# More expert-row dots among the query pieces, fewer behind them, and a smoother ramp of GpSimd's row requests

## The reference

```python
def peer_ffn(h, w_q, subkeys, u, v):
    def chunk(ht):
        q = (ht @ w_q).reshape(128, 8, 2, 128)
        s = jnp.einsum('thpc,hpnc->thpn', q, subkeys)
        sv, si = lax.top_k(s, 16)
        cand_s = sv[:, :, 0, :, None] + sv[:, :, 1, None, :]
        cand_i = si[:, :, 0, :, None] * 128 + si[:, :, 1, None, :]
        top_s, top_pos = lax.top_k(cand_s.reshape(...), 16)
        expert = jnp.take_along_axis(cand_i.reshape(...), top_pos, axis=-1)
        gate = jax.nn.softmax(top_s, axis=-1)
        act = gelu(jnp.einsum('thkd,td->thk', u[expert], ht))
        return jnp.einsum('thk,thkd->td', gate * act, v[expert])
    return lax.map(chunk, hc)
```

## Time and profile before

| | before |
|---|---|
| median of 3 runs | 2679.6 us (2672.1 to 2680.65) |
| the profiled execution | 2673.85 us, its span 2672.1 us |
| TensorE busy | 2589.0 us (97%) |
| VectorE busy | 2137.8 us (80%) |
| GpSimd busy | 1497.7 us (56%) |
| ScalarE busy | 883.2 us (33%) |
| moved by DMA | 763.33 MB |

### The profile page before, as it was taken

The page is one execution under the profiler, slowest core; times in us unless marked ns, Lnnn a source line. Parts: engine busy times, 40 slices in busy tenths (PEclk is TensorE's granted clock), DMA queues, the critical chain, the costliest instruction groups (busy, mean ns, idle before and its releaser), DMA issues.

```text
span 2672.1 us, 41571 instructions
## 1 busy us (share of the span) xinstructions
PE 2589.0 (97%) x15177; PEld 2324.3 (87%) x15177; DVE 2137.8 (80%) x4585; ACT 883.2 (33%) x1656; POOL 1497.7 (56%) x960
## 2 busy tenths in 40 slices
PE   7999989999999999999999999999999999999998
PEld 6777767999999999999999999987888788888886
DVE  6122273589888899999999996769898899989998
ACT  4223252222222222236666664222222222222222
POOL 1111020245666677776655656846776677767763
PEclk9999999999999999999999999999999999999999
DMA  4110023335777899999999999999999999999995
GB/s 149 48 32 25 24 62 121 111 107 166 266 271 268 295 318 325 319 328 365 385 373 380 383 372 375 406 359 366 388 383 387 370 385 385 387 386 376 385 375 220
DMA packets 296526, 763.33 MB, mean 286 GB/s; under 512 B 25808, under 2 KB 116304, under 8 KB 293584
## 3 DMA queue, kind: packets, MB, share of 16 engines
q0 software_dynamic: 110592, 402.70, 40.2%
q1 hardware_dynamic: 161280, 288.88, 31.3%
q10 hardware_dynamic: 24528, 70.26, 6.8%
HBM read 669.47 MB, written 92.27 MB: 285 GB/s over the span
## 4 chain that ended last, share of the span: by engine, by line
PE 61%; DVE 12%; DMA 7%; issue 4%; POOL 2%; ACT 1%; SPq 0%; DVEq 0%; ACTq 0%
PE bank L1659 27%; PE bank L2048 12%; PE wide L2048 9%; PE bank L2019 5%; DMA g_raw<-g_d 4%; PE bank L1879 3%; PE bank L1934 2%; DVE u_row L1393 2%; DMA u_row<-in_v,ids 1%; DVE v_lo L1610 1%; DVE yg L1603 1%; DVE eq L1463 1%; PE bank L1943 1%; DVE a_lo L1567 1%; POOL w_lo L686 1%
## 5 line engine op out<-in xcount | busy, mean ns | idle before, releaser
L745 POOL DMA_INDIRECT d_row<-in_v,ids x344 | 599.4, 1742 | 272.4 <-DVE yg L1603 190.4
L1659 PE MATMUL bank<-h_hi,w_hi 128*128 128x320 f32 (+1 forms) x2368 | 562.0, 318 | 13.4 <-POOL w_lo L686 11.2
L1659 PE MATMUL bank<-h_hi,w_lo 128*128 128x320 f32 (+1 forms) x2368 | 545.2, 312 | 1.0 <-issue 1.0
L1659 PE MATMUL bank<-h_lo,w_hi 128*128 128x320 f32 (+1 forms) x2368 | 544.5, 311 | 0.0
L686 POOL TENSOR_TENSOR w_lo<-w_raw,w_hi 128x1024 fp32r<-128x1024 f32 x144 | 356.7, 2477 | 286.1 <-ACT w_hi L968 209.1
L1393 DVE CUSTOM_DVE_ANT_0 u_row<-wide,u_row 128x1024 f32<-128x1024 f32 x384 | 449.5, 1220 | 22.7 <-DMA u_row<-in_u_rows,ids 10.9
L697 POOL DMA_INDIRECT u_row<-in_u_rows,ids x384 | 385.5, 1004 | 109.9 <-issue 79.3
L1603 DVE SCALAR_TENSOR_TENSOR yg<-d_row,uh,yg 128x1024 f32<-128x1024 f32 x344 | 426.3, 1277 | 1.0
L1659 PEld LDWEIGHTS bank<-h_hi,w_hi 128*128 128x128 f32 x2368 | 392.1, 189 | 19.6 <-ACT act_st L962 8.9
L1659 PEld LDWEIGHTS bank<-h_lo,w_hi 128*128 128x128 f32 x2368 | 398.3, 188 | 2.5
L1659 PEld LDWEIGHTS bank<-h_hi,w_lo 128*128 128x128 f32 x2368 | 397.1, 188 | 3.6 <-issue 1.1
(11 more groups left out here) (225 smaller groups left out, 4297.0 us busy)
## 6 DMA issues: line engine op xcount, KB each, us to landing
w_raw<-in_u SPq DMA_DIRECT2D x128, 512.0 KB
v_raw<-in_v ACTq DMA_DIRECT2D x126, 512.0 KB
act_d<-act_st SPq DMA_DIRECT2D x128, 320.0 KB
g_d<-g_st SPq DMA_DIRECT2D x20, 2048.0 KB
a_raw<-act_d SPq DMA_DIRECT2D x154, 256.0 KB
g_raw<-g_d SPq DMA_DIRECT2D x120, 256.0 KB
w_raw<-in_w_q SPq DMA_DIRECT2D x32, 512.0 KB
w_raw<-in_w_in SPq DMA_DIRECT2D x20, 512.0 KB
```

The lines of the kernel that those rows point to most:

```text
L745: nc.gpsimd.indirect_dma_start(d_row[k % DR][:, :], None, v_rows, bass.IndirectOffsetOnAxis(ids[:, c:c + 1], 0)).then_inc(d_in[k % DR], 16)
L1659: ins = pe.matmul(banks[h][:, 0:n], lhs[:, part], rhs[:, k, h * n:(h + 1) * n], start=(k == 0 and lhs is lhs_hi and rhs is h_hi), stop=(k ...
```

## The change

The rows are dealt out in another way:

- The query pieces have 2, 4, 6, 6, ... 6 dots, 90 for 80. A piece's dots are halved between its two halves of `top_keys`.
- A tile has 22 early rows instead of 20, so 428 rows are done before the product stage and 340 in it. Groups 1 to 4 there have 21 late rows instead of 22.
- Stretch C has 428 - 372 = 56 rows where it had 424 - 362 = 62. GpSimd asks for 6 per body instead of 7.
- `rows_by` follows the new counts. In the first three items behind the query pieces (44, 45, 46) it is 5, 3 and 1 less; and in items 8 to 10 GpSimd asks for 2, 3 and 4 rows ahead instead of 5.

```diff
-ROWS_QUERY = 5
+QUERY_ROWS = (2, 4) + (6,) * (Q_PIECES - 2)
-ROWS_Q = 2 * ROWS_EARLY + ROWS_QUERY * Q_PIECES
+ROWS_Q = 2 * ROWS_EARLY + sum(QUERY_ROWS)
...
-ROWS_BODY_C = 7
-EARLY = 20
+ROWS_BODY_C = 6
+EARLY = 22
...
+ROWS_UNIT_FULL = (2, 2, 2, 2, 2, 3, 2, 2, 2, 2)
+FULL_GROUPS = 4
...
-    if g == 0:
-        return sum(ROWS_UNIT0[:u])
-    per_unit = ROWS_UNIT if g + 1 < NG else ROWS_UNIT_LAST
-    return sum(ROWS_UNIT0) + sum(ROWS_UNIT) * (min(g, NG) - 1) + (
-        sum(per_unit[:u]) if g < NG else sum(ROWS_UNIT_LAST) - sum(ROWS_UNIT))
+    by_group = [ROWS_UNIT0, *[ROWS_UNIT_FULL] * FULL_GROUPS, *[ROWS_UNIT] * (NG - FULL_GROUPS - 2), ROWS_UNIT_LAST]
+    return sum(sum(rows) for rows in by_group[:g]) + (sum(by_group[g][:u]) if u else 0)
...
                 if t < 2 * BODY1:
-                    return min(max(2 * (t - Q_ITEM0), 0), 2 * ROWS_EARLY) + ROWS_QUERY * max(t - Q_ITEM0 - 2, 0) // 2
-                return ROWS_Q + (ROWS_FRONT - ROWS_Q) * (t - 2 * BODY1) // (2 * B0 - 2 * BODY1)
+                    hp, part = divmod(max(t - Q_ITEM0 - 2, 0), 2)
+                    return (min(max(2 * (t - Q_ITEM0), 0), 2 * ROWS_EARLY) + sum(QUERY_ROWS[:hp])
+                            + part * QUERY_ROWS[hp] // 2)
+                behind = max(5 - 2 * (t - 2 * BODY1), 0)
+                return ROWS_Q + (ROWS_FRONT - ROWS_Q) * (t - 2 * BODY1) // (2 * B0 - 2 * BODY1) - behind
...
                 if t >= GATHER_ITEM:
-                    gathers_u(rows_by(t) + 5)
+                    gathers_u(rows_by(t) + min(2 + t - GATHER_ITEM, 5))
...
-                    for r in range((ROWS_QUERY + 1 - q) // 2):
+                    for r in range((QUERY_ROWS[hp] + 1 - q) // 2):
                         dot_row()
```

## The result

| | kernel before | changed kernel |
|---|---|---|
| median of 6 runs, us | 2675.59 (2672.1 to 2680.65) | 2658.06 (2656.75 to 2661.17) |
| profiled execution, its span, us | 2673.85, 2672.1 | 2659.01, 2657.2 |

The ratio is 0.9934, with a 95% interval of 0.9923 to 0.9945: faster by 17.5 us. The forecast was a gain of 9.65 us, 2670.0 us, range 2660 to 2679.5. The sign was right; the gain was mis-sized, and the result lies 1.9 us under the range. In a later set with eleven runs of the kernel before (median 2676.3), five more of the changed kernel gave 0.9929 (0.9913 to 0.9945).

The account below looks back on a forecast made before the run. TensorE was taken to bound nearly all of the kernel, so gains come only from its idle places. Terms -2.3, +1.15, -5.7, +1.0 and -3.8 sum to -9.65 us: 2679.6 to 2670.0 us, range 2660 to 2679.5.

Parts of the forecast that it names:

- Stretch C: Last chunks before the product stage: fewer GpSimd requests per chunk cut TensorE's 7.2 us idle to 1.5, -5.7 us.
- The start of the query pieces: First query pieces: two dots fewer ahead of VectorE's key search shorten TensorE's wait for ix, -2.3 us.
- Pays nothing: Items 8 to 10: the request ramp removes a 1.83 us w_lo wait, but TensorE only reaches VectorE's wait earlier.
- I take that as kept: Behind the ix wait: 2.2 us of lower clock stays, since 3.3 us of idle remains.
- The query pieces and behind them: Ten more dots fit VectorE's waits; the last piece's extra dot delays TensorE behind the pieces, +1.15 us.
- all that TensorE gains at 913 it loses by 957: Behind the query pieces: the 2.76 us wait goes, but a VectorE dot still sets the later start at 957.
- The second rival: Stretch C is not relieved because requests beside early rows take longer; -5.7 is lost, 2675.7 us, chance 0.17.
- The new wait for the last rows: First product waits 0 to 2.8 us for the last-requested row, none with the request queue gone; taken as +1.0 us.
- The product stage, -3.8: A row less in groups 1 to 4 removes the 2113 wait, 1.91 us plus 1.93 of clock; the 1948 wait stays.
- The third rival: Product stage: its wait only moves to another group; sum -5.85, 2673.8 us, chance 0.20.
- Its sign of being wrong: Product stage: the forecast is wrong if waits for y return behind group 5.
- The slower rival: Query pieces: VectorE overruns its 1.2 us room per piece when rows land late; +21 us, 2691 us, chance 0.06.

Follow-up runs that it names:

- e1: Kernel before, with GpSimd asking for 2, 3 and 4 rows ahead in items 8 to 10 instead of 5: 2672.36 us beside 2677.23 for the kernel before.
- e6: Kernel before, with GpSimd asking for 6 instead of 7 rows per body in stretch C, its 62 rows there unchanged: 2666.26 us.
- e3: Changed kernel without the term that holds back the early-row requests of items 44 to 46: 2655.22 us.
- e5: Changed kernel with GpSimd again asking for 7 rows per body in stretch C, 56 rows in all: 2669.15 us.
- e4: Changed kernel with groups 1 to 4 back at 22 late rows and the last group at 23 instead of 27: 2656.87 us.

## Why the prediction was right, and where it was wrong

**What bounds the kernel: right.** TensorE bounds it, and the gain came out of its idle places and of the clock behind them.

**The start of the query pieces: the term that failed.** It said -2.3 us; items 8 to 52 gave -2.10 - 8.58 = -10.7. A wait of 2.76 us in there is the next paragraph's, which leaves 7.9. The rows divide that: 1.83 us (the wait for w_lo at 632.83), 3.78 - 0.81 = 2.97 (the wait for ix), and 16.28 - 14.08 = 2.2 us of clock in the two chunks behind it; 0.9 us is not placed. Three statements of that step failed. "Pays nothing", of the ramp: it made VectorE itself 2.8 us quicker (e1), since w_lo no longer ran into its eq. "3.3 us", for the wait left: 2.3 us for the two dots held (e1 to the changed kernel, 3.10 to 0.81 us, is 2.29), but it was to be taken from a wait that the ramp had not lengthened. And so "I take that as kept", of the clock: with 0.81 us of idle it did not fall. I had written that 2.2 us more would be gained if it went; I didn't ask what would make it go.

How much the term should have been is less certain than these statements, for the start is not the same in two executions of the kernel before. Against e6, items 8 to 52 gave 7.6 us, without the 2.76 some 4.8. The term was too small against either, but up to 3 us of the 7.9 are the profiled execution's and not the change's.

**The query pieces and behind them: size near, one statement wrong.** VectorE waits 1.25 us a piece (forecast 1.2), the pieces stay at 15.2 us. The wait at item 45 went (-2.76) and a wait at item 51 grew to 3.07 from 1.00 and 0.67, with the clock at 0.83 in the 10 us around it. Together -2.76 + 2.69 = -0.07, forecast +1.15. A second wait, at item 47, did not come. That a dot of VectorE sets the start of item 51 in the changed kernel is in GpSimd's timeline, where the w_lo follows this request and one more:

```profile
944.12 0.94 POOL L696 DMA_INDIRECT u_row<-in_u_rows,ids  x1 [6.82 <-DVE uh L1395]
```

But "all that TensorE gains at 913 it loses by 957" is not borne out: without the holding back the wait at item 45 is 4.00 us, and item 51 starts 2.6 us later (e3). The edit of items 44 to 46, which the sum counts as nothing, is worth 2.0 us.

**Stretch C: right, a little short.** Idle time fell from 7.20 to 1.91 us (forecast 1.5 left). e5 undoes this one number and loses 8.1 us there, so it is the rate of requests that counts, and three to a chunk nearly tie, as forecast. The second rival is out: w_lo took 2510 ns and the requests 1329 and 1244 in the groups there (2443, 1279 and 1031 in the earlier trace rows), a little longer each but with three to a chunk no delay:

```profile
L701 POOL DMA_INDIRECT u_row<-in_v,ids x35 | 46.5, 1329 | 8.9 <-issue 7.5 <-DVE uh L1395 0.9 <-DVE yg L1410 0.3
L685 POOL TENSOR_TENSOR w_lo<-w_raw,w_hi 128x1024 fp32r<-128x1024 f32 x15 | 37.7, 2510 | 0.3
L696 POOL DMA_INDIRECT u_row<-in_u_rows,ids x9 | 11.2, 1244 | 2.3 <-issue 1.8 <-DVE uh L1395 0.3
```

**The new wait for the last rows, +1.0: not there.** The first product waits 3.97 us for a_lo in both kernels. The last request did move as worked out: it stood 3.4 us ahead of the last w_hi and now stands 2.5 us behind it, 6.0 us later in the order of the work (forecast 4.9). What was too dear is the way from request to use: 7.1 us (1742.41 to 1749.50), not the 14.3 us of the earlier trace rows. My other end, "the queue gone", was the true one, and it gives no wait. The mechanism is real where rows are left over for the end: 10.58 us in e6.

**The product stage, -3.8: right where it was meant, and hidden in the whole.** The wait at 2113 and that at 1948 are gone, as said, the second against the forecast. From the 25th v_hi to TensorE's end the stage takes 4.6 us less, and with the rows put back (e4) it is 747.3 us again. The third rival ("only moves") is out for these waits. What the prediction has no term for is the start of the stage, ahead of the 25th v_hi: 7.3 us longer in the first profile, 2.5 in the second. There the wait of 2.93 us at 1777 stood where 0.88 stood; it was 2.31 in e1, which has the old stretch C and the old counts, so the shorter C is not shown to cause it. Its sign of being wrong, waits for y behind group 5, did not come: behind 1895 the changed kernel and the six runs that share its counts have 0 to 1.5 us of idle time each, the four with 22 rows 2.2 to 4.3.

**The slower rival** did not come: the DMA share rose from 0.75 to 0.86 in the query pieces, and VectorE kept its 1.25 us a piece there, with no wait for a row among its waits of 700 to 900 us:

```profile
DVE top L1361 <- PE bank L1945: 16.1, 13, 1.3
```

**The number.** The forecast for the median missed by 11.9 us. The sum missed 5.2 us of the 14.8 between the profiled executions, stage by stage 6.8 us in the front (items 8 to 84), 1.3 in the strips (chance), 2.1 in C with its end, 1.4 behind TensorE's end (chance), and 6.5 the other way in the products. Up to 4.0 of the 6.8 are the front of one execution of before. Another 4.0 us are the base: the median of three runs from which the forecast counted, 2679.6, is 2675.6 with six. The last 2.7 us lie between the gain of the medians, 17.5, and that of the profiled executions. That the sum of stages came near was in part luck: the front's miss and the loss at the start of the products have opposite signs. The profiled execution, 2673.85, was the better base, and the range, which had to hold both, should have reached below 2660: its low end left out that the ramp could speed VectorE up and that the clock could come with it.

## What to carry to other kernels

When one engine's work is moved off a second's, price both sides of the encounter: here a late w_lo on GpSimd made VectorE's instruction beside it 2 us longer, and its cure was counted as nothing because only TensorE's wait was looked at. Where a wait in the trace has cost the clock too, ask what would shorten it enough, since both then go together. And before a stage is tuned by one profile, run the same program again: here the product stage differs by 4 to 10 us by itself, and a front without the ramp by 4. A mark in the middle of a stage then helps: the part behind it repeated within 2.4 us, and showed an effect of 4.6 us that the whole stage hid.
